# Neighbourhood attention over latent tokens kept in column order, each query tile against its neighbouring key tiles

## The reference

```python
rs = jnp.clip(r - wr // 2, 0, rows - wr)                 # rows = wr = 8: every row is in the window
cs = jnp.clip(col - NA_WIN_COLS // 2, 0, GRID_W - NA_WIN_COLS)
in_win = (col[None, :] >= cs[:, None]) & (col[None, :] < cs[:, None] + NA_WIN_COLS)   # 16 of 64 columns
...
s_loc = jnp.einsum('brqhd,brwkhd->bhrqwk', qg, kg).astype(jnp.float32) * NA_SCALE + bias
s_loc = jnp.where(in_win[:, None, :], s_loc, -jnp.inf)
s_ctx = jnp.einsum('brqhd,blhd->bhrql', qg, k_ctx).astype(jnp.float32) * NA_SCALE
...
p = jax.nn.softmax(s, axis=-1).astype(v.dtype)           # over local keys and 128 cached context keys
o = jnp.einsum('bhrqwk,brwkhd->brqhd', p_loc, vg) + jnp.einsum('bhrql,blhd->brqhd', p_ctx, v_ctx)
```

## Time and profile before

| | us |
|---|---|
| median of 3 runs | 2993.45 (2991.03 to 3000.39) |
| the profiled execution | 3000.19 |
| its span, first to last instruction | 2998.6 |
| one trip of the head loop | 40.06 |
| mean granted clock of TensorE | 0.976 of 2.4 GHz |

### The profile page before, as it was taken

The page is one execution under the profiler, slowest core; times in us unless marked ns, Lnnn a source line. Parts: engine busy times, 40 slices in busy tenths (PEclk is TensorE's granted clock), DMA queues, the critical chain, the costliest instruction groups (busy, mean ns, idle before and its releaser), DMA issues.

```text
span 2998.6 us, 42056 instructions
## 1 busy us (share of the span) xinstructions
PE 2864.5 (96%) x15862; PEld 2514.7 (84%) x15862; DVE 1920.8 (64%) x2943; ACT 1053.4 (35%) x1815; POOL 167.9 (6%) x203
## 2 busy tenths in 40 slices
PE   7899999999898999599999999999999999999997
PEld 2688888877777777499999999999999978888885
DVE  8766667485776596766666666666666555424338
ACT  7422333234443211644444444444444312212121
POOL 0200111000000000000000000000000000000005
PEclk9999999999998999799999999999999999999998
DMA  9854333351222654222222222222222444224231
GB/s 390 288 188 144 128 117 135 104 192 60 101 91 90 233 190 146 91 102 98 97 97 97 100 102 102 97 97 97 97 97 100 164 134 159 95 78 148 77 126 71
DMA packets 104151, 384.05 MB, mean 128 GB/s; under 512 B 13142, under 2 KB 13290, under 8 KB 102010
## 3 DMA queue, kind: packets, MB, share of 16 engines
q1 hardware_dynamic: 89088, 317.36, 29.7%
q0 software_dynamic: 14240, 65.03, 6.2%
q10 hardware_dynamic: 730, 0.38, 0.0%
HBM read 351.20 MB, written 35.21 MB: 129 GB/s over the span
## 4 chain that ended last, share of the span: by engine, by line
PE 85%; DVE 8%; DMA 3%; ACT 2%; issue 1%; ACTq 0%; DVEq 0%; SPq 0%
PE ps L1870 15%; PE ps L1872 15%; PE ps L1871 14%; PE ps L2328 12%; PE ps L2329 12%; PE ps L2330 12%; DMA mraw<-in_wstream 2%; DVE acc L1322 1%; PE ps L2060 1%; PE ps L2033 1%; PE ps L2017 1%; DVE wlo L1294 1%; DVE mx L1410 1%; ACT whi L867 0%; DVE mlo L1345 0%
## 5 line engine op out<-in xcount | busy, mean ns | idle before, releaser
L2328 PE MATMUL ps<-acth,ringh 128*128 128x320 f32 x2464 | 762.3, 309 | 17.4 <-DVE ringl L1694 17.4
L2329 PE MATMUL ps<-actl,ringh 128*128 128x320 f32 x2464 | 762.2, 309 | 0.0
L2330 PE MATMUL ps<-acth,ringl 128*128 128x320 f32 x2464 | 762.1, 309 | 0.0
L2328 PEld LDWEIGHTS ps<-acth,ringh 128*128 128x128 f32 x2464 | 463.3, 188 | 17.8 <-DVE ringl L1694 17.8
L2329 PEld LDWEIGHTS ps<-actl,ringh 128*128 128x128 f32 x2464 | 463.2, 188 | 0.0
L2330 PEld LDWEIGHTS ps<-acth,ringl 128*128 128x128 f32 x2464 | 463.2, 188 | 0.0
L1870 PE MATMUL ps<-dwh,fring 128*128 128x512 f32 x820 | 320.3, 391 | 8.5 <-DVE acc L1807 7.6
L1872 PE MATMUL ps<-dwh,fring 128*128 128x512 f32 x820 | 319.9, 390 | 0.0
L1871 PE MATMUL ps<-dwl,fring 128*128 128x512 f32 x820 | 319.9, 390 | 0.0
L1781 DVE TENSOR_TENSOR dwl<-raw,dwh 128x1024 fp32r<-128x1024 f32 x82 | 100.4, 1224 | 306.9 <-ACT dwh L1260 306.9
L1294 DVE TENSOR_TENSOR wlo<-raw,whi 128x1024 fp32r<-128x1024 f32 x111 | 138.0, 1244 | 242.8 <-ACT whi L867 242.5
(11 more groups left out here) (299 smaller groups left out, 4996.8 us busy)
## 6 DMA issues: line engine op xcount, KB each, us to landing
raw<-in_wstream SPq DMA_DIRECT2D x503, 512.0 KB, 3.3
mraw<-in_wstream SPq DMA_DIRECT2D x64, 512.0 KB, 7.6
fscr<-fst POOLq DMA_DIRECT2D x44, 320.0 KB, 2.4
fst<-fscr SPq DMA_DIRECT2D x21, 640.0 KB, 4.4
acc<-in_xT SPq DMA_DIRECT2D x8, 640.0 KB, 18.3
oscr<-ost POOLq DMA_DIRECT2D x16, 320.0 KB, 2.5
ostage<-oscr POOLq DMA_DIRECT2D x16, 320.0 KB, 5.8
acc<-in_xtok POOLq DMA_DIRECT2D x1, 5120.0 KB, 17.8
```

The source lines that it names most:

```text
L2328: mm(out, ringh[:, s, w], ah, start=first, stop=False, skip_group_check=True)
L2329: mm(out, ringh[:, s, w], al, start=False, stop=False, skip_group_check=True)
L2330: ins = mm(out, ringl[:, s, w], ah, start=False, stop=last, skip_group_check=True)
```

## The change

The latent tokens are kept in another order: tile `t` holds the columns 16t to 16t + 15 of all 8 rows. The window of 16 columns then reaches only into the tile itself and its neighbours: tiles 0 and 3 meet two key tiles, 1 and 2 three (`KEY0`, `KEY1`, `NEAR`). Scores, bias, maximum, exponential, scaling, transposes and the copy to `PT` are cut to these; the product with V takes for each key tile only the queries that see it. The block of `PT` that key tile 1 has for query tile 3 is set to zero once, so that this product may cover all queries.

The new order is made where DVE scales the activations: it writes `pb[:, k % 3]` through a permuting view instead of `xstage` in place. The residual, the rotary table and the mask are loaded in strips of 16 partitions, one for each row of the grid, and `y` is stored through a strided view. The bias goes through two tables in DRAM (`tbl`, then `near`), and POOL adds the mask in three instructions.

```diff
+KEY0 = [max(t - 1, 0) for t in range(LT)]
+KEY1 = [min(t + 2, LT) for t in range(LT)]
+NEAR = [(KEY1[t] - KEY0[t]) * P for t in range(LT)]
+BIAS_AT = [0, 2 * P, 2 * P, 5 * P]
+BIAS = 7 * P
+COLS = GRID // LT
...
-    tbl = nc.dram_tensor("tbl", (NH, P, 14 * GRID), f32, kind="Internal").ap()
+    tbl = nc.dram_tensor("tbl", (NH, COLS, 2 * WR - 1, 3 * COLS), f32, kind="Internal").ap()
+    near = nc.dram_tensor("near", (NH, P, 3 * P), f32, kind="Internal").ap()
...
+        def by_column(x, w):
+            return x.rearrange("p (j r c) -> p r j c", j=LT, r=WR) if w else x.rearrange("p (r j c) -> p r j c", r=WR, j=LT)
...
+            pool.memset(PT[:, 1, 3 * P:4 * P], 0.0).then_inc(unit_set, 1)
...
+            for r in range(WR):
+                for u in range(2):
+                    pool.dma_start(ropet[r * COLS:(r + 1) * COLS, u, :, :],
+                                   rope[r % 2 * GRID:(r % 2 + 1) * GRID, u, r // 2, :].rearrange(
+                                       "(j c) e -> c j e", j=LT)).then_inc(early_in, 16)
+            pool.wait_ge(early_in, 16 * (3 + 2 * WR))
...
             for a in range(NH):
-                for r in range(2):
-                    src = bass.AP(tensor=rpbpad.tensor, offset=PAD + WC - 1 + a * RPB + (1 - r) * (2 * WC - 1),
-                                  ap=[[2 * WC - 1, 14], [-1, GRID], [1, GRID]])
-                    pool.dma_start(tbl[a, r * GRID:(r + 1) * GRID, :].rearrange("p (j k) -> j p k", j=14),
-                                   src).then_inc(tbl_in, 16)
+                src = bass.AP(tensor=rpbpad.tensor, offset=PAD + a * RPB - 1,
+                              ap=[[2 * WC - 1, 2 * WR - 1], [-1, COLS], [1, 3 * COLS]])
+                pool.dma_start(tbl[a].rearrange("c m x -> m c x"), src).then_inc(tbl_in, 16)
+            pool.wait_ge(tbl_in, 16 * NH)
+            for a in range(NH):
+                src = bass.AP(tensor=tbl.tensor, offset=(a * COLS * (2 * WR - 1) + WR - 1) * 3 * COLS,
+                              ap=[[(2 * WR - 1) * 3 * COLS, COLS], [-3 * COLS, WR], [1, 3 * P]])
+                pool.dma_start(near[a].rearrange("(r c) x -> c r x", r=WR), src).then_inc(tbl_in, 16)
...
-            pool.dma_start(capx, cap).then_inc(na_consts_in, 16)
+            for r in range(WR):
+                for q, k, n, o in ((0, 0, 2, 0), (1, 0, 3, 2), (3, 2, 2, 5)):
+                    pool.dma_start(capx[r * COLS:(r + 1) * COLS, o * COLS:(o + n) * COLS],
+                                   cap[q * COLS:(q + 1) * COLS, k * COLS:(k + n) * COLS]).then_inc(na_consts_in, 16)
...
+            pool.wait_ge(na_consts_in, 16 * NA_CONSTS)
+            pool.wait_ge(tbl_in, 32 * NH)
...
-                pool.dma_start(TB, tbl[a]).then_inc(tb_in, 16)
+                pool.dma_start(rawt, near[a]).then_inc(tb_in, 16)
                 pool.wait_ge(tb_in, a * 16 + 16)
-                nc.gpsimd.tensor_tensor(TB, TB, capx, ALU.add).then_inc(tb_ready, 1)
+                w = rawt.rearrange("p (r d c) -> p d r c", r=WR, d=3)
+                for o, d, n in ((0, 1, 2), (2, 0, 3), (5, 0, 2)):
+                    c = capx[:, o * COLS:(o + n) * COLS].rearrange("p (d c) -> p d c", d=n)
+                    ins = nc.gpsimd.tensor_tensor(TB[:, o * P:(o + n) * P].rearrange("p (d r c) -> p d r c", d=n, r=WR),
+                                                  w[:, d:d + n], c.unsqueeze(2).to_broadcast([P, n, WR, COLS]), ALU.add)
+                ins.then_inc(tb_ready, 1)
...
-                    pool.dma_start(xs, xtok).then_inc(xs_in, 16)
+                    for r in range(WR):
+                        pool.dma_start(xs[r * COLS:(r + 1) * COLS, 0:LT, :],
+                                       xtok[r % 2 * GRID:(r % 2 + 1) * GRID, r // 2, :].rearrange(
+                                           "(j c) e -> c j e", j=LT)).then_inc(xs_in, 16)
+                    pool.dma_start(xs[:, LT, :], xtok[:, LT, :]).then_inc(xs_in, 16)
...
-                pool.dma_start(y[t], xs[:, t, :]).then_inc(y_out, 16)
+                out = bass.AP(tensor=y.tensor, offset=t * COLS * D, ap=[[GRID * D, WR], [D, COLS], [1, D]])
+                pool.dma_start(out, xs[:, t, :]).then_inc(y_out, 16)
...
-                             (ropet[:, :, :, :], rope), (bcols[:, :], bcol)):
+                             (bcols[:, :], bcol)):
...
-                nc.scalar.activation(hh[:, k, :], xstage[:, k, :], ACT.Copy).then_inc(h_hi, 1)
+                nc.scalar.activation(hh[:, k, :], pb[:, k % 3, :], ACT.Copy).then_inc(h_hi, 1)
...
-                        nc.scalar.activation(pb[:, s % 3, LAT:T], ps[5][:, 0:CTX], ACT.Copy,
+                        nc.scalar.activation(pb[:, s % 3, NEAR[s]:NEAR[s] + CTX], ps[5][:, 0:CTX], ACT.Copy,
...
-                        nc.scalar.activation(PT[:, 0:4, t * P:(t + 1) * P],
-                                             ps[6][:, :].rearrange("p (k q) -> p k q", k=4), ACT.Copy)
+                        k0, k1 = (KEY0[t], KEY1[t]) if na else (0, LT)
+                        nc.scalar.activation(PT[:, k0:k1, t * P:(t + 1) * P],
+                                             ps[6][:, 0:(k1 - k0) * P].rearrange("p (k q) -> p k q", q=P), ACT.Copy)
...
-                        nc.scalar.activation(pb[:, s % 3, :], pb[:, s % 3, :], ACT.Exp, bias=nb, scale=1.0,
+                        v = pb[:, s % 3, 0:NEAR[s] + CTX]
+                        nc.scalar.activation(v, v, ACT.Exp, bias=nb, scale=1.0,
...
-                for lo, hi, c in ((0, LAT, 0), (LAT, T, 1)):
-                    ins = V.tensor_scalar(xstage[:, k, lo:hi], xstage[:, k, lo:hi], mod1[:, KD + k, c:c + 1],
-                                          mod1[:, k, c:c + 1], ALU.mult, ALU.add)
+                if k >= 3:
+                    dve.wait_ge(h_ready, k - 2)
+                for dst, src, c in ((by_column(pb[:, k % 3, 0:LAT], True), by_column(xstage[:, k, 0:LAT], False), 0),
+                                    (pb[:, k % 3, LAT:T], xstage[:, k, LAT:T], 1)):
+                    ins = V.tensor_scalar(dst, src, mod1[:, KD + k, c:c + 1], mod1[:, k, c:c + 1], ALU.mult, ALU.add)
...
-                V.tensor_tensor(hl[:, k, :], xstage[:, k, :], hh[:, k, :].bitcast(f32), ALU.subtract).then_inc(h_ready, 1)
+                V.tensor_tensor(hl[:, k, :], pb[:, k % 3, :], hh[:, k, :].bitcast(f32), ALU.subtract).then_inc(h_ready, 1)
...
-                        own.link(V.scalar_tensor_tensor(out=pb[:, r, 0:LAT], in0=ps[4][:, :], scalar=NA_SCALE,
-                                                        in1=TB[:, (6 - 2 * s) * GRID:(14 - 2 * s) * GRID],
+                        own.link(V.scalar_tensor_tensor(out=pb[:, r, 0:NEAR[s]], in0=ps[4][:, 0:NEAR[s]], scalar=NA_SCALE,
+                                                        in1=TB[:, BIAS_AT[s]:BIAS_AT[s] + NEAR[s]],
...
-                        own.link(V.reduce_max(mx[:, r, 2:3], pb[:, r, :], AX.X))
+                        own.link(V.reduce_max(mx[:, r, 2:3], pb[:, r, 0:NEAR[s] + CTX], AX.X))
...
-                    n = T if t < LT else CTX
+                    n = CTX if t == LT else NEAR[t] + CTX if na else T
...
+            dve.wait_ge(early_in, 16 * (3 + 2 * WR))
...
+                        dve.wait_ge(xs_in, 16 * (WR + 1))
...
-                            mm(ps[bk][:, :], qT[:, o], kT[:, 0:LAT], start=True, stop=True)
+                            mm(ps[bk][:, 0:NEAR[s]], qT[:, o], kT[:, KEY0[s] * P:KEY1[s] * P], start=True, stop=True)
...
-                            for k in range(4):
+                            n = NEAR[t] if na else LAT
+                            for k in range(n // P):
                                 nc.tensor.transpose(ps[6][:, k * P:(k + 1) * P], pb[:, t % 3, k * P:(k + 1) * P], idt[:, :])
...
-                            nc.tensor.transpose(last, pb[:, t % 3, LAT:T], idt[:, :]).then_inc(pt_ready, 1)
+                            nc.tensor.transpose(last, pb[:, t % 3, n:n + CTX], idt[:, :]).then_inc(pt_ready, 1)
...
-                    for k in range(5):
-                        mm(ps[bk][:, :], vh[:, k, :], PT[:, k, :], start=(k == 0), stop=(k == 4))
+                    if na:
+                        mm(ps[bk][:, :], vh[:, LT, :], PT[:, LT, :], start=True, stop=False)
+                        for k in (0, 2, 3):
+                            mine = [t for t in range(LT) if KEY0[t] <= k < KEY1[t]]
+                            q = slice(mine[0] * P, (mine[-1] + 1) * P)
+                            mm(ps[bk][:, q], vh[:, k, :], PT[:, k, q], start=False, stop=False)
+                        mm(ps[bk][:, :], vh[:, 1, :], PT[:, 1, :], start=False, stop=True)
+                    else:
+                        for k in range(5):
+                            mm(ps[bk][:, :], vh[:, k, :], PT[:, k, :], start=(k == 0), stop=(k == 4))
```

24 lines of the change are left out of this document (11 added, 13 removed).

## The result

The changed kernel takes 3011.25 us (median of seven, 3009.55 to 3015.90) against 2991.76 for the kernel before on the same chip: a ratio of 1.006, 95% interval 1.0043 to 1.0077. The forecast was 2970.3 us and faster; it became 19.5 us slower. The profiled execution has a span of 3009.7 us, against 2998.6 before.

The account below looks back on a forecast made before the run. PE, 96% busy, was taken to bound the kernel; -24.2 (work) - 1.3 (wait) + 1.0 (table) + 0.3 (scalings) + 1.0 (residual) = -23.2 us, from the median 2993.45 to 2970.3, range 2963 to 2999.

Parts of the forecast that it names:

- What PE loses: Head loop: fewer columns in scores, transposes and product with V take 3.02 us a head off PE, 24.2 for eight.
- the wait: Head loop, before tile 0's transposes: PE's wait for tile 1's maximum falls from 0.22 to about 0.04, 1.3 us more.
- rival (e): Behind the head loop: a lower-clock stretch of PE shortens, more gain than the sum, under 2964 us; chance 0.04.
- The bias table: First bias table: moves from 163.1 to about 176 us, at worst 181; DVE wants it at 251.6, so all hidden.
- The prologue: Kernel start: rotary table and first scaled activations add 1.0 and 0.3 us; its end at most 3 us later.
- the table: Prologue: rotary table as 16 loads of 16 partitions in 256 B runs costs 0 to 2.7 us, taken as 1.0.
- the scalings: Start of the V projection: three scalings writing runs of 16 into a buffer of three cost 0.3 us, or 0.
- The residual: Output projection: residual in strips lands later and PE idles as much longer; 1 us likeliest, bounds 0 and 47.
- (a): The forecast itself, at the output projection: the residual's strips cost under 4 us, 2965 to 2974; chance 0.38.
- Rival (c): Output projection: strips go at about a third of the residual's rate, 28.5 us more, 2989 to 3002; chance 0.20.
- The output stores: Kernel end: the output stores keep their size and row length, SP's context-tile stores end behind them; no cost.
- rival (d): Output projection: strips at a quarter of the rate, 42.7 us more, gain more than gone, 3014 us; chance 0.08.

Follow-up runs that it names:

- the wide version: The changed kernel with residual in one transfer, output tiles stored as 128 rows in a row, rotary table in one transfer, all arranged on the host: 2970.44 us, ratio 0.9932.

## Why the prediction was wrong, point by point

**What PE loses: right.** The forecast was 3.02 us a head and 0.18 a trip for the wait, 25.5 in all. A trip got 3.17 shorter. From the seventh head's product with V (at 502.46, and at 522.87 before) to the eighth's (578.85, 603.95) the gain was 4.69 instead, but the kernel before itself needs 81.08 us for this stretch in one profile and 79.50 in another, so the 1.5 above the trip's gain are not the change's; part of rival (e)'s subject, the stretch at the lower clock, lies in it. With the eighth product's own 1.06 and the later start of 0.84 the loss of work comes to 27.0, and to 25.5 without those 1.5. The wait was sized right and read wrong: I took the 0.22 in the row of the four transposes for it, and that stays (0.44 for two); what went is the 0.20 of PE's idle time ahead of the row. The bias table stayed hidden: it was ready at 168.9, and DVE first used it at 251.9.

**The prologue: near in size, its parts not.** 1.0 for the table and 0.3 for the scalings were forecast. The table cost 1.4 (93.50 against 92.12), the scalings gained 0.3 instead, and PE started 0.84 later.

**The residual: this step failed.** I had 1.0 us with bounds 0 and 47; measured is 28.2 in landing (17.8 to 46.0) and about 27 to 32 in time, from both sides: added to the kernel before it costs 26.9 by the medians and 31.7 by the ratio, taken from the changed one it gives 28.5 and 27.8. Two readings led there. First, for the rate of a 16-partition load I took rows of loads that write to all 128 partitions, the 512 KB weight tile of 3.3 us above all; it is equal in bytes and differs in the one thing that was new. A strip of that size among its like takes 39.4 / 8 = 4.9 us. Second, I read the share of 0.99 at 424 GB/s as "nothing but the engines limited it" and so as a ground for (a). The share says that engines have packets under way, not how fast these go: at 166 GB/s it was 0.99 too. Rival (c) had the size (28.5 more), and the Trainium skill's page that I weighed and set aside (SBUF — State Buffer, Door 1) had its reason, with 26 more as an estimate; it deserved the place of (a), since that page spoke of this very kind of transfer and no row of the trace did.

**The output stores: a term was left out.** "The output stores keep their size and row length ... Nothing." They kept both, and lost the form of their address in memory. That is 7.0 to 7.5 us in the tail of the profiles, and 3.9 to 9.8 by ratios and medians.

**The sum again.** By the medians the wide version is 23.0 faster; the strips cost 28.5, the stores 9.8, and the table 4.6: -23.0 + 28.5 + 9.8 + 4.6 = 19.9, and 19.5 was measured. That it closes so well is partly luck. By the ratios the same terms are -20.3 + 27.8 + 3.9 + 3.9 = 15.3 against 18.0, and for the stores and the table only the profiles separate the cost from none, with 7.5 and 1.4. Even with the strips priced right the forecast would have been 2998 and "no change"; of the 13 us from there to 3011 the stores' tail is the largest part that a profile shows, and it is not the mechanism of rival (d), whose strips would have had to be slower still.

**The span and the median.** The profiled execution of before stood 6.7 us over its median, without a place for it in my text. The second attention alone differs by 11 us between two profiles of the same code, which is enough for it.

## What to carry to other kernels

A new order of tokens can cost something at every place where the old order meets memory: list all loads and stores that it touches, and price each by its partitions per transfer and its slowest dimension, not by bytes and row length. Keep each transfer as wide as the tile (or spread over every fourth partition), and arrange the rows where it is free, ahead of the kernel. When a transfer is to be cut, ask what stands behind it in its queue: here 28 us of slow load became 25 to 32 us of idle PE, in part because the next small reload was behind it in the queue and in part because the engines were busy for any queue.

## What the hardware showed that I had not expected

- The busy share of the DMA engines was 0.99 to 1.00 at 390 GB/s and at 155 to 166. It cannot show whether a transfer is well formed; the GB/s beside it can.
- Equal bytes into 16 neighbouring partitions, 16 spread, 32 neighbouring, 32 spread: 43, 31, 32 and 20 us.
- A queue of its own for the slow load brought PE's wait from 32.4 us only to 18.1.
- One slow store slowed plain stores of another queue beside it: SP's took 7.3 us to land instead of 3.6, and 1.86 to issue instead of 0.34.
- The same code between 725 and the last product with V took 237 us in one profile and 226 in another, with PE at a granted clock of 0.94 and 0.98 from 690 to 930.
